# Modulation weights in wide strips between the memory products, memory rows first, gla_q's two tiles side by side

## The reference

```python
c_act = jax.nn.silu(c)                                    # (1, 2048)
mod = (c_act @ ada_w[l] + ada_b[l]).reshape(B, 6, D)      # ada_w: 2048 x 12288
shift_m, scale_m, gate_m, shift_f, scale_f, gate_f = ...
h = rmsnorm(x, norm_mix_g[l]) * (1.0 + scale_m) + shift_m
# token_mix: h @ w_in, whose first 1024 columns are GLA's q, then k, v, g, the gate's rank-16 input ...
# second block, in each of its two layers:
kv = rmsnorm_2(mem, mem_g) @ w_mem_kv                     # mem: 256 x 2048, w_mem_kv: 2048 x 1024
```

## Time and profile before

| | us |
|---|---|
| median of 3 runs | 2947.26 (2947.05 to 2947.93) |
| profiled execution, span of its instructions | 2939.3 |
| what lies around the span, against the median | 8.0 |
| PE busy | 2794.3 |
| DVE busy | 1771.9 |
| ACT busy | 1211.5 |
| first matmul of mem_k0 | 71.98 |
| first matmul of gla_k | 258.52 |

### The profile page before, as it was taken

The page is one execution under the profiler, slowest core; times in us unless marked ns, Lnnn a source line. Parts: engine busy times, 40 slices in busy tenths (PEclk is TensorE's granted clock), DMA queues, the critical chain, the costliest instruction groups (busy, mean ns, idle before and its releaser), DMA issues.

```text
span 2939.3 us, 45956 instructions
## 1 busy us (share of the span) xinstructions
PE 2794.3 (95%) x19494; PEld 2585.1 (88%) x19494; DVE 1771.9 (60%) x2201; ACT 1211.5 (41%) x1625; POOL 10.9 (0%) x21
## 2 busy tenths in 40 slices
...
GB/s 345 292 243 209 296 151 87 270 279 271 251 243 218 101 120 253 283 172 207 181 187 186 194 182 182 185 201 157 173 186 148 184 147 186 182 181 172 73 115 128
DMA packets 320675, 574.67 MB, mean 196 GB/s; under 512 B 22127, under 2 KB 61367, under 8 KB 319112
## 3 DMA queue, kind: packets, MB, share of 16 engines
...
q10 hardware_dynamic: 470, 0.16, 0.0%
...
## 4 chain that ended last, share of the span: by engine, by line
PE 85%; DVE 10%; ACT 2%; issue 2%; DMA 1%; ACTq 0%; SPq 0%; DVEq 0%
PE tile_ps L877 77%; PE misc_ps L877 7%; DVE w_lo L1767 4%; DVE probs_t L1834 1%; ACT w_hi L1361 1%; DMA w_raw<-in_ada_w 1%; PE misc_ps L1061 1%; DMA w_raw<-in_w_mem_kv 0%; DVE stats L2036 0%; DVE gla_var L2194 0%; DVE o_hi L2020 0%; DVE nsa_probs L2032 0%; DVE o_lo L2021 0%; DVE o_hi L1881 0%; DVE qk L2200 0%
## 5 line engine op out<-in xcount | busy, mean ns | idle before, releaser
L1767 DVE TENSOR_TENSOR w_lo<-w_raw,w_hi 128x1024 fp32r<-128x1024 f32 x866 | 1021.0, 1221 | 936.3 <-ACT w_hi L1361 935.2
L1361 ACT ACTIVATE w_hi<-w_raw 128x1024 fp32r<-128x1024 f32 x866 | 868.5, 1051 | 1222.4 <-PE tile_ps L877 1199.5
L877 PE MATMUL tile_ps<-h_hi,w_hi 128*128 128x256 f32 x3952 | 656.3, 287 | 45.8 <-DVE w_lo L1767 29.3
L877 PE MATMUL tile_ps<-h_hi,w_lo 128*128 128x256 f32 x3952 | 646.1, 285 | 0.0
L877 PE MATMUL tile_ps<-h_lo,w_hi 128*128 128x256 f32 x3952 | 646.1, 285 | 0.0
L877 PEld LDWEIGHTS tile_ps<-h_hi,w_hi 128*128 128x128 f32 x3952 | 554.9, 194 | 54.0 <-issue 32.5
L877 PEld LDWEIGHTS tile_ps<-h_lo,w_hi 128*128 128x128 f32 x3952 | 552.9, 194 | 0.0
L877 PEld LDWEIGHTS tile_ps<-h_hi,w_lo 128*128 128x128 f32 x3952 | 552.8, 194 | 0.0
L1834 DVE SCALAR_TENSOR_TENSOR probs_t<-w_raw,c_act,probs_t 128x512 f32<-128x512 f32 x330 | 247.7, 750 | 18.3 <-DMA w_raw<-in_ada_w 8.8
L877 PE MATMUL tile_ps<-w_hi,h_hi 128*128 128x512 f32 x352 | 110.2, 394 | 1.5 <-DVE w_lo L1767 1.5
L877 PE MATMUL tile_ps<-w_hi,sw_hi 128*128 128x512 f32 x352 | 108.7, 390 | 0.3 <-DVE w_lo L1767 0.2
...
## 6 DMA issues: line engine op xcount, KB each, us to landing
w_raw<-in_ada_w SPq DMA_DIRECT2D x96, 1024.0 KB, 5.2
w_raw<-in_w_in SPq DMA_DIRECT2D x89, 1024.0 KB, 5.1
w_raw<-in_ffn_w_in SPq DMA_DIRECT2D x88, 1024.0 KB, 5.0
w_raw<-in_w_out SPq DMA_DIRECT2D x48, 1024.0 KB, 5.1
w_raw<-in_ffn_w_down SPq DMA_DIRECT2D x44, 1024.0 KB, 5.1
w_raw<-in_b_w_in SPq DMA_DIRECT2D x33, 1024.0 KB, 5.2
w_raw<-in_a_w_in SPq DMA_DIRECT2D x32, 1024.0 KB, 5.4
w_raw<-in_w_kv SPq DMA_DIRECT2D x24, 1024.0 KB, 5.2
```

Of the source, the lines that this page charges most:

```text
L877: return nc.tensor.matmul(o, l, r, start=start, stop=stop, skip_group_check=True)
L1361: f(w_hi[s_ % 2][:, hf], w_raw[r % 4][:, hf], ACT.Copy).then_inc(cut_hi, 1)
L1767: ins = v.tensor_tensor(w_lo[s_ % 2][:, hf], w_raw[r % 4][:, hf], f32(w_hi[s_ % 2][:, hf]), ALU.subtract)
```

## The change

Same bytes and the same number of slots before gla_k; another order, another shape of the modulation slots, and another division of their work.

- The products ada0 and ada1 and the riders of the memory products go. In their place stand three strips of the shift and the scale columns together: columns 0 to 511, 512 to 1535 and 1536 to 2047 of both parts, so 1024, 2048 and 1024 columns wide. A slot of strips 0 and 2 holds two contraction chunks of 1024 columns, loaded as two transfers of 512 KB; a slot of strip 1 holds one chunk of 2048 columns in one transfer. They are 8 + 16 + 8 slots.
- mem_rows is loaded right after the constants; behind it come slots (0,0) to (0,4) of strip 0, then the memory products with strip slots between their pieces, as AFTER says, and the rest of the strips between gla_q's first six pieces. x is loaded behind the first piece of mem_v0.
- PE takes slots 0, 2 and 4 of strip 0 with the weights stationary and c_act moving (16 matmuls of one column each), straight into the columns of the sums; DVE takes the other 29 (strip_piece). strip_total stands in mem_v0, after mem_v1 and in gla_q (8, 16 and 8 matmuls). ada_row, row_out and turn_row go.
- gla_q's tiles go side by side (across=True): pieces (0,0), (1,0), (0,1), (1,1) and so on.
- mix_chunk and mix_low: chunks 0 to 3 in mem_v1, 4 to 7 and 8 to 11 after the first and second entry of gla_q's between, 12 to 15 after the sixth. turn_x starts one piece later and ends in mem_v1; the squares of x move from mem_k0 to mem_v0.
- ACT makes c_act after seven of its vector loads, not after all.
- Some small buffers move; later products and their riders are as before.

```diff
-ADA_COL = [0, 4, 1, 5, 2, 6, 3, 7]
-PRODUCTS = [Product("ada0", 2, 4, split=False, mode="A", rider=1, on_pe=(1,)),
-            Product("ada1", 2, 4, split=False, mode="A", rider=1, on_pe=(1,)),
-            Product("mem_k0", 1, 4, rider=1), Product("mem_v0", 1, 4, mode="N", rider=1),
-            Product("mem_k1", 1, 4, rider=1), Product("mem_v1", 1, 4, mode="N", rider=1),
-            Product("gla_q", 2, 4), Product("gla_gk", 1, 1, kc=16, width=P),
+STRIPS = ((0, 512), (512, 1024), (1536, 512))
+STRIP_PE = (0, 2, 4)
+STRIP_TILES = 8
+def strip_chunks(s):
+    return 1024 // STRIPS[s][1]
+AHEAD_OF_ALL = [(0, n) for n in range(5)]
+AFTER = {"mem_k0": [[(0, 5)], [(0, 6)], [(0, 7)], [(1, 0)]],
+         "mem_v0": [[(1, 1)], [(1, 2)], [(1, 3)], [(1, 4)]],
+         "mem_k1": [[(1, 5)], [(1, 6)], [(1, 7)], [(1, 8)]],
+         "mem_v1": [[(1, 9)], [(1, 10), (1, 11)], [(1, 12), (1, 13)], [(1, 14), (1, 15)]],
+         "gla_q": [[(2, 0), (2, 1)], [(2, 2)], [(2, 3), (2, 4)], [(2, 5)], [(2, 6)], [(2, 7)], [], []]}
+PRODUCTS = [Product("mem_k0", 1, 4), Product("mem_v0", 1, 4, mode="N"),
+            Product("mem_k1", 1, 4), Product("mem_v1", 1, 4, mode="N"),
+            Product("gla_q", 2, 4, across=True), Product("gla_gk", 1, 1, kc=16, width=P),
...
             sp.dma_start(const[:], A["const"]).then_inc(ld_const, 16)
+            sp.dma_start(mem_rows[:], mem_in.rearrange("(t p) d -> p t d", p=P)).then_inc(ld_mem, 16)
...
+            def load_strip(s, n):
+                r, (c0, w), nc_ = STRIP_RING[s, n], STRIPS[s], strip_chunks(s)
+                if r >= 4:
+                    free_slot(G["mem_k0"], 0, r)
+                dst = w_raw[r % 4][:].rearrange("p (c a n) -> p c a n", c=nc_, a=2)
+                src = ada_w[:, :, 0:2 * D].rearrange("p c (a n) -> p c a n", a=2)[:, :, :, c0:c0 + w]
+                for c in range(nc_):
+                    sp.dma_start(dst[:, c], src[:, n * nc_ + c]).then_inc(landed[r % 4], 16)
...
-                        if g.mode == "A":
-                            load_ada(g, i, tb, q)
-                            if ring(g, tb, q) == 5:
-                                sp.dma_start(mem_rows[:], mem_in.rearrange("(t p) d -> p t d", p=P)).then_inc(ld_mem, 16)
-                            if ring(g, tb, q) == 15:
-                                sp.dma_start(x[:], x_in.rearrange("(t p) d -> p t d", p=P)).then_inc(ld_x, 16)
-                            continue
...
+                        if name in AFTER:
+                            if name == "mem_v0" and e == 0:
+                                sp.dma_start(x[:], x_in.rearrange("(t p) d -> p t d", p=P)).then_inc(ld_x, 16)
+                            for s, n in AFTER[name][e]:
+                                load_strip(s, n)
+            for s, n in AHEAD_OF_ALL:
+                load_strip(s, n)
+            for name in ("mem_k0", "mem_v0", "mem_k1", "mem_v1"):
...
-            def ada_on_pe(g, q):
-                r, t = ring(g, 1, q), 0 if g.name == "ada0" else 1
...
+            def strip_on_pe(n):
+                r = STRIP_RING[0, n]
                 pe.wait_ge(landed[r % 4], LANDED[r])
+                w = w_raw[r % 4][:].rearrange("p (c n) -> p c n", c=2)
+                for c in range(2):
+                    k = 2 * n + c
+                    for b in range(8):
+                        last = mm(strip_sums(0, b), w[:, c, b * P:(b + 1) * P], c_act[:, k:k + 1], k == 0 and b == 0, False)
+                last.then_inc(strip_by_pe, 1)
+            def strip_total(s):
+                pe.wait_ge(strip_step, strip_ops(s, 16 // strip_chunks(s) - 1) + strip_chunks(s))
+                if s == 2:
+                    pe.wait_ge(mod_ready, 1)
+                for b in range(2 * STRIPS[s][1] // P):
+                    last = mm(strip_sums(s, b), strip_acc[s][:, b * P:(b + 1) * P], ones[:, 0:1], s > 0, True)
+                last.then_inc(strip_sum, 1)
...
-            ada0, ada1 = G["ada0"], G["ada1"]
-            ada_on_pe(ada0, 0)
-            ada_on_pe(ada0, 1)
+            strip_on_pe(0)
             turn_vectors()
-            ada_on_pe(ada0, 2)
-            ada_on_pe(ada0, 3)
             to_features(0)
-            ada_on_pe(ada1, 0)
             to_features(1)
-            ada_on_pe(ada1, 1)
+            strip_on_pe(2)
             to_features(2)
-            early_total(ada0, bank[3])
-            ada_on_pe(ada1, 2)
             to_features(3)
-            ada_on_pe(ada1, 3)
+            strip_on_pe(4)
             for b in range(2):
                 pe.wait_ge(turn_out[b], 2)
             h, h_mem = (of(h_hi), of(h_lo)), (of(mem_hi), of(mem_lo))
             o = (of(o_hi), of(o_lo))
             done = lambda n: [(nm_lo, N[n].c0 + N[n].n)]
             as_normed = lambda n: (lambda k: [(nm_lo, N[n].c0 + k + 1)])
-            product("mem_k0", *h, chunk_ready=as_normed("mem0"), total=False,
-                    between=[lambda: early_total(ada1, bank[3]), lambda: turn_row(0), lambda: turn_row(1)])
-            product("mem_v0", *h, total=False, between=[lambda: early_total(G["mem_k0"], bank[2])])
-            product("mem_k1", *h_mem, chunk_ready=as_normed("mem1"), total=False,
-                    between=[lambda: (early_total(G["mem_v0"], bank[2]), turn_x(0), turn_x(1))] +
-                    [lambda j=j: (turn_x(2 * j), turn_x(2 * j + 1)) for j in range(1, 4)])
-            product("mem_v1", *h_mem, total=False, between=[lambda: early_total(G["mem_k1"], bank[3], 1)])
-            product("gla_q", *h, chunk_ready=as_normed("mix"), between=[lambda: early_total(G["mem_v1"], bank[3])])
+            product("mem_k0", *h, chunk_ready=as_normed("mem0"))
+            product("mem_v0", *h, between=[lambda: strip_total(0)])
+            product("mem_k1", *h_mem, chunk_ready=as_normed("mem1"),
+                    between=[None] + [lambda j=j: (turn_x(2 * j), turn_x(2 * j + 1)) for j in range(3)])
+            product("mem_v1", *h_mem, between=[lambda: (turn_x(6), turn_x(7)), None, None, lambda: strip_total(1)])
+            product("gla_q", *h, chunk_ready=as_normed("mix"), between=[None] * 5 + [lambda: strip_total(2)])
...
+                    if n_vec == 7:
+                        act.wait_ge(c_turned, 1)
+                        f(c_act[:], bank[0][:, 0:DC], ACT.Silu).then_inc(c_ready, 1)
...
-            product("mem_k0", copy_to(lambda i, tb, g: mem_k_out[:, 0]), between=[lambda: (row_out(1), second[0]())] + [lambda j=j: (second[j](), x_squares(j - 1)) for j in range(1, 4)])
+            product("mem_k0", copy_to(lambda i, tb, g: mem_k_out[:, 0]), between=second[:4])
             product("mem_v0", copy_to(lambda i, tb, g: mem_v_out[:, 0]),
-                    between=[lambda: (second[4](), x_squares(3)), second[5], lambda: (second[6](), sums("mix")), second[7]])
+                    between=[second[4], lambda: (second[5](), x_squares(0), x_squares(1)),
+                             lambda: (second[6](), x_squares(2)), lambda: (second[7](), x_squares(3))])
             product("mem_k1", copy_to(lambda i, tb, g: mem_k_out[:, 1]),
-                    between=[lambda j=j: (x_leaves(2 * j), x_leaves(2 * j + 1)) for j in range(4)])
+                    between=[lambda: sums("mix")] + [lambda j=j: (x_leaves(2 * j), x_leaves(2 * j + 1)) for j in range(3)])
             product("mem_v1", copy_to(lambda i, tb, g: mem_v_out[:, 1]),
-                    between=[lambda j=j: [mix_chunk(3 * j + c) for c in range(3)] for j in range(4)])
+                    between=[lambda: (x_leaves(6), x_leaves(7)), lambda: [mix_chunk(c) for c in range(4)]])
             stored = [(st_mkv, 64)]
             pair = lambda c0: (lambda i, tb, g: qk[:, bass.ds(per(i, 2 * g.body) + 2 * tb, 2), c0:c0 + 2, :])
-            product("gla_q", copy_to(pair(0), scale=GLA_DK ** -0.5), between=[lambda: [mix_chunk(c) for c in range(12, DC)]])
+            product("gla_q", copy_to(pair(0), scale=GLA_DK ** -0.5), between=[lambda: [mix_chunk(c) for c in range(4, 8)], lambda: [mix_chunk(c) for c in range(8, 12)],
+                             None, None, None, lambda: [mix_chunk(c) for c in range(12, DC)]])
...
+                                for s, n in AFTER[name][e - 1] if name in AFTER else ():
+                                    strip_piece(s, n)
...
+            def strip_piece(s, n):
+                r, nc_, ops = STRIP_RING[s, n], strip_chunks(s), strip_ops(s, n)
+                first = next(m for m in range(8) if s or m not in STRIP_PE)
+                w = w_raw[r % 4][:].rearrange("p (c n) -> p c n", c=nc_)
+                acc = strip_acc[s]
+                dve.wait_ge(landed[r % 4], LANDED[r])
+                if s == 2 and n == 0:
+                    dve.wait_ge(strip_sum, 1)
+                for c in range(nc_):
+                    k = n * nc_ + c
+                    if n == first and c == 0:
+                        ins = v.tensor_scalar(acc, w[:, c, :], c_act[:, k:k + 1], None, ALU.mult)
+                    else:
```

(52 more changed lines are left out.)

127 lines of the change are left out of this document (54 added, 73 removed).

## The result

The changed kernel takes 2919.61 us (median of 4 runs, 2918.50 to 2926.05), the kernel before 2947.30 (4 runs, 2947.05 to 2947.93): a ratio of 0.9919, 95% interval 0.9907 to 0.9931, so 0.81% faster. The forecast was 2912, range 2901 to 2930, faster. The direction and the mechanism held, and the range holds the time. But the traces show a gain of 21.0 us up to gla_k where I had worked out 35.3. That the forecast still lies only 7.6 us off the median is in part luck: a second miss, in how I went from the span to the median, hides half of the first.

The account below looks back on a forecast made before the run. TensorE, busy 95% of the span, was taken as the bound, so only its idle time could be won. Stage terms -31.0 - 12.5 + 1.7 - 2.4 + 1.1 + 0 + 7.8 gave -35.3 us: 2912 us, range 2901 to 2930.

Parts of the forecast that it names:

- PE starts at its lower level ... I take 5.3: Start: strip piece 0 on PE at 1.2 of 2.4 GHz takes between 3.2 and 6.4 us, taken as 5.3.
- Two to_features (1.8 each, as the same 16 records of turn_x): Start, behind the norm: two to_features at 1.8 us each, then strip piece 2 (3.2) and two more, until 34.2.
- one slot: Start: constants and one slot had landed at 13.4 before; memory rows replace slots and land at about 13.4.
- mem_k0, mem_k1, gap, gla_gk: Stage terms: mem_k0 12.5 us less, mem_k1 2.4 less, gap to gla_q 0 (9.3 again), gla_gk as now, 6.7.
- The rival that wide operations cost as their columns do: DVE's strip operations cost 750 ns per 512 columns, giving 2919 us; chance 0.12.
- I take 2.5: mem_v0: loading x takes 5.4 us of queue, partly covered; 2.5 taken between bounds 0 and 5.4.
- at 0.95: mem_v1: four mixed chunks on DVE at 0.95 us each, behind the cut of piece 2, end at 14.0.
- 8.4 + 7 x 5.8: gla_q: one cold piece of 8.4 us and seven of 5.8, plus 10.5 of waits: 59.5, 7.8 more.
- The split loads: Rival: 16 slots arriving as two 512 KB transfers each come 1.3 us late, 21 us in all: 2933; chance 0.08.
- a span of 2939.3 us with 8.0 around it: Last step: profiled span 2939.3 against median 2947.26, so 2939.3 - 35.3 + 8.0 = 2912 us.
- The slower rival: Late strips hold up DVE's cuts; 1.2 us for each of 29 cancels the gain, 2.4 gives 2981; slower 0.05, same 0.04.

Follow-up runs that it names:

- fillers: Changed kernel plus eight spare 512-column matmuls on PE ahead of strip slot (0,0) and two behind the transposes of the vectors: 2915.85 us, ratio 0.9901.
- narrow operations: Changed kernel with each of DVE's strip operations cut into operations of 512 columns: 2923.23 us, ratio 0.9927.
- the loads early: Changed kernel with gla_q's loads issued by SP ahead of its wait for mem_v1: 2915.63 us, ratio 0.9894.
- the stores late: Changed kernel with GpSimd's four stores of the memory's k and v waiting until gla_q is done: 2920.66 us, ratio 0.9914.

## Why the prediction was right, and where its terms were off

**Start: mis-sized, -22.8 for -31.0.** The step "PE starts at its lower level ... I take 5.3", and behind it "Two to_features (1.8 each, as the same 16 records of turn_x)". Slot (0,0) took 6.96, the diagonals were ready at 25.33 and not 23.8, and the chain of to_features, slot, to_features took 16.8 us where I had 10.4; the tail on DVE was 7.0 for 6.8. I took the price of turn_x from the middle of a product, where PE is warm, and let PE start cold once. It is slow for most of the stretch. The fillers gave 5.0 of the 8.2 us back, and 3.7 to 4.0 came and went between executions of the same PE instructions, with the granted clock (0.58 and 1.00 in the windows above). The landing of the memory rows was forecast well, 12.87 for 13.4, though "one slot" is a slip: by 13.47 two slots had landed before, and these are the 2 MiB that the rows replace.

**mem_k0, mem_k1, gap, gla_gk: right** within 0.3 us, and with them the price of the wide operations. The rival that wide operations cost as their columns do is dead by 2347 and 1282 ns; built by hand, as narrow operations, it costs some 3 us.

**mem_v0: -0.5 for +1.7.** "I take 2.5" for x's part of the queue. It ran at 392 GB/s, more than any stage before, and ACT waited for its weights twice (78.67, 2.72 us). In other executions with the same loads in this stage it took from 23.6 (with the fillers) over 24.2 and 25.0 to 27.8 us; with x loaded earlier 23.6 in four of four. So x costs 0 to 4.2 us there, and the sum's 2.5 was a fair middle for a term that varies.

**mem_v1: mis-sized, +3.7 for +1.1.** The wait is where it was forecast, ahead of the last piece, 3.66 us for 2.8. The 0.9 us came from DVE's cut of the third piece, which ended 12.1 us into the stage (139.2) and not 11.2. Its four mixed chunks then took 2.9 us: my text has them "at 0.95", which would be 3.8, but my step from 11.2 to 14.0 took 2.8. What I left out is what follows the wait: the last piece takes 7.37 for 5.5.

**gla_q: mis-sized, +13.1 for +7.8.** The waits are 9.95 in all for the 8.9 of my steps, but they are not where I put them, so this agreement is in part luck. PE waited 1.85 ahead of the second piece, where I had none; 3.97 for 2.4 ahead of the third; 2.04 for 4.6 ahead of the fourth; 2.09 for 1.9 ahead of the last pair. I had let DVE alone set them. But ACT waited 6.94 and 4.16 us for the weight slots of the second and third piece, which share the queue with 16 strip transfers and the stores of the memory. The larger term is again what follows a wait. In gla_q PE is busy 54.84 us where my eight pieces and the total make 50.6: "8.4 + 7 x 5.8" has one cold piece, and in fact the piece behind 3.97 us of waiting took 8.35 us (1.23 for its first four records, 0.74 behind 2.04), and the last pair, behind 2.09, 13.24 for 11.6. The forecast wait of 4.6 us alone should have put a second 2.4 us there. With the loads early the same stage still took 63.9, and with the stores late 64.2, so neither the stores nor the late first load is the cause of its length by itself. Two candidates remain, and neither was tried alone: the order in which DVE makes chunks, strips and cuts, and weight slots that land late even with the loads early (3.94 us of ACT's waiting in the row above).

**The split loads: no loss seen.** While only 512 KB transfers were in flight, at 15.6 to 22.5 us, the queue moved 376 GB/s at a DMA share of 1.02, where the whole stage before had 351 to 353. By the Trainium skill (DMA: Bandwidth & Descriptors, section Rules for kernel authors) a transfer should be at least 1 MiB for full bandwidth; this trace doesn't bear it out for several transfers in flight: half of that came within 3% of the 386 of the earlier trace rows. A transfer of 512 KB took 7.5 us to land in the median, one of 1024 KB 5.2 over the whole run and 6.7 in the first 250 us. A slot in one transfer, for comparison, wasn't tried.

**From the span to the time: wrong, and it helped.** "a span of 2939.3 us with 8.0 around it". What lies around a span is 1.7 to 2.0 us in every execution that reports both (2920.01 for 2918.2). The other 6 were no fixed part: the profiled execution of before was a shorter one than the median. Other executions of that kernel have spans of 2936.7 to 2946.6. So the stages' miss of 14.3 us came out as 7.6. That the medians lie 27.7 apart and the traces 21.0 is the same thing seen from the other side: a single execution can lie 6 us and more from its kernel's median, and one of the places is the 3.8 us behind gla_k shown above.

**The slower rival** (strips hold up the cuts, 1.2 us for each of 29) has its mechanism in the trace at five places, at 1.9 to 4.0 us each: 13.6 us of waits in mem_v1 and gla_q together, part of them for late weight slots. It bears on the size of the gain, far from its sign.

## What to carry to other kernels

Price a small matmul by the clock that PE will have where it is put, and not by the same instruction in the middle of a product: here a pair of to_features took 3.66 to 6.35 us. Add to a forecast wait on PE what the piece behind it loses. In gla_q of these thirteen traces the pieces behind waits of 2.9 to 9.4 us took 7.5 to 8.7 us, those behind 0.5 to 1.9 took 6.0, and those behind 2.0 to 2.5 one or the other. A few spare matmuls in a hole that is there anyway gave 2.4 to 5 us. And before a sum is set against a median, look how far single executions of the kernel lie apart: here up to 10 us for the kernel before and 7 to 8 for the changed one, a third of the change.

## What the runs showed of the chip

TensorE's granted clock fell to 0.58 with PE's records free of holes, in a stretch of 128-column and one-column matmuls ahead of which it had been idle for 2.1 us, and in another execution of the same PE instructions, with the transfer of x beside them, it stayed at 1.00; in a third, with that transfer too, it fell to 0.61. In the first microseconds behind a long hole the records are slow while the granted clock still reads 1.00: slot (0,0) took 217 ns a matmul at 15.58, against 113 for the same number of such records once warm (3.63 us for 32, slot (0,2) with the fillers). No run shows why. Behind the same wait of 2.09 us, with the one-column matmuls of strip_total ahead of it, gla_q's last pair of pieces took 13.24 us in three traces and 14.1 to 14.5 in eight. And whole executions fall into classes: in the 20 us that begin 200 us behind gla_k's start the clock is 1.00 or 0.83, and from gla_k to the end they take 2680.2 to 2680.8 or 2684.1 to 2684.6 us, with nothing between in thirteen traces.
